# A differential-attention and SSM block on one core: TensorE turns the identity before x is ready, and two groups of waits move to later matmuls

## The reference

```
h = rmsnorm(x, g_mix);  proj = h @ w_in            # 1024 -> q, k, v, u, gate_a, gate_s
attn = diff_attention(q, k, v, rel_bias, lam, subln_g)     # 8 heads, two softmaxes each
y = s5_ssm(u, ...)                                  # diagonal state space, 32 groups
z = gelu(y) @ w_glu;  ssm = z_val * sigmoid(z_gate)
x = x + (sigmoid(gate_a) * attn + sigmoid(gate_s) * ssm) @ w_out
h = rmsnorm(x, g_mlp)
x = x + square(relu(h @ w1)) @ w2
return rmsnorm(x, g_final)
```

## Time and profile before

| | us |
|---|---|
| median of 3 runs | 754.74 (754.58 to 755.03) |
| profiled execution, its own time | 753.81 |
| span of the profiled execution | 752.0 |
| PE busy in the span | 739.0 |
| first PE instruction starts | 6.78 |
| first matmul of the first projection starts | 14.46 |

### The profile page before, as it was taken

The page is one execution under the profiler, slowest core; times in us unless marked ns, Lnnn a source line. Parts: engine busy times, 40 slices in busy tenths (PEclk is TensorE's granted clock), DMA queues, the critical chain, the costliest instruction groups (busy, mean ns, idle before and its releaser), DMA issues.

```text
span 752.0 us, 10173 instructions
## 1 busy us (share of the span) xinstructions
PE 739.0 (98%) x3826; PEld 618.0 (82%) x3826; DVE 506.8 (67%) x952; ACT 360.9 (48%) x630; POOL 54.1 (7%) x51
## 2 busy tenths in 40 slices
PE   6999999999999999999999999999999999999996
PEld 5878888888888888888888888888888888888885
DVE  4669998776667873546752576756676567647687
ACT  7524632256667664642332655434453345335455
POOL 2210000000000100000001000011000200010005
PEclk9999999999999999999999999999999999999999
DMA  7674339952224431326339563788277835795322
GB/s 248 196 164 121 93 112 173 173 143 72 71 71 127 155 113 45 89 91 224 107 90 254 134 145 85 188 241 193 64 158 244 209 104 112 196 260 131 84 58 112
DMA packets 99505, 106.19 MB, mean 141 GB/s; under 512 B 10540, under 2 KB 68576, under 8 KB 98432
## 3 DMA queue, kind: packets, MB, share of 16 engines
q1 hardware_dynamic: 93120, 87.05, 40.8%
q0 software_dynamic: 5504, 16.78, 12.0%
q10 hardware_dynamic: 832, 1.71, 1.1%
HBM read 89.70 MB, written 5.34 MB: 126 GB/s over the span
## 4 chain that ended last, share of the span: by engine, by line
PE 98%; DMA 0%; DVE 0%; ACT 0%; issue 0%; DVEq 0%
PE ps L1703 29%; PE ps L1704 29%; PE ps L1705 29%; PE ps L2018 3%; PE ps L1991 2%; PE ps L2008 1%; PE ps L1779 1%; PE ps L1787 1%; PE ps L1910 1%; PE ps L1894 1%; PE ps L1871 0%; PE ps L1914 0%; DMA mixA<-in_x 0%; PE ps L1786 0%; PE ps L1882 0%; PE ps L1859 0%
## 5 line engine op out<-in xcount | busy, mean ns | idle before, releaser
L1703 PE MATMUL ps<-hT_hi,w_hi 128*128 128x512 f32 x384 | 151.0, 393 | 0.3 <-DVE hT_lo L1038 0.3
L1705 PE MATMUL ps<-hT_hi,w_lo 128*128 128x512 f32 x384 | 149.7, 390 | 0.0
L1704 PE MATMUL ps<-hT_lo,w_hi 128*128 128x512 f32 x384 | 149.5, 389 | 0.0
L1703 PE MATMUL ps<-w_hi,hT_hi 128*128 128x512 f32 x288 | 113.7, 395 | 0.0
L1705 PE MATMUL ps<-w_hi,hT_lo 128*128 128x512 f32 x288 | 112.3, 390 | 0.0
L1704 PE MATMUL ps<-w_lo,hT_hi 128*128 128x512 f32 x288 | 112.1, 389 | 0.0
L1498 DVE TENSOR_TENSOR w_lo<-raw,w_hi 128x1024 fp32r<-128x1024 f32 x78 | 94.5, 1221 | 22.9 <-ACT w_hi L906 21.5
L906 ACT ACTIVATE w_hi<-raw 128x1024 fp32r<-128x1024 f32 x78 | 81.7, 1052 | 56.2 <-PE ps L1705 56.2
L664 ACT ACTIVATE w_hi<-raw 128x1024 fp32r<-128x1024 f32 x62 | 64.2, 1058 | 56.5 <-PE ps L1705 51.2
L1703 PE MATMUL ps<-w_hi,fa_hi 128*128 128x512 f32 x224 | 87.1, 389 | 0.0
L1704 PE MATMUL ps<-w_lo,fa_hi 128*128 128x512 f32 x224 | 87.1, 389 | 0.0
(11 more groups left out here) (271 smaller groups left out, 1030.9 us busy)
## 6 DMA issues: line engine op xcount, KB each, us to landing
raw<-in_w SPq DMA_DIRECT2D x64, 512.0 KB, 4.7
raw<-in_w_in SPq DMA_DIRECT2D x44, 512.0 KB, 5.0
raw<-raw POOLq DMA_DIRECT2D x8, 1024.0 KB, 7.1
raw<-in_w_glu SPq DMA_DIRECT2D x8, 512.0 KB, 3.8
raw<-in_w_out SPq DMA_DIRECT2D x8, 512.0 KB, 3.8
T_w<-in_w SPq DMA_DIRECT2D x8, 512.0 KB, 6.9
T_w<-in_w POOLq DMA_DIRECT2D x8, 512.0 KB, 7.7
raw<-in_w POOLq DMA_DIRECT2D x8, 512.0 KB, 6.8
```

The source lines that it names most:

```text
L1703: nc.tensor.matmul(dst, a_hi, b_hi, start=start, stop=False)
L1704: nc.tensor.matmul(dst, a_hi, b_lo, start=False, stop=False)
L1705: return nc.tensor.matmul(dst, a_lo, b_hi, start=False, stop=stop)
```

## The change

There are three edits, all in PE's list. First, a new helper turn_identity turns the identity onto itself, into a place of PSUM that the turning of x overwrites later: 24 times as soon as the identity is there, before the wait for the first block of x, and 8 times before the wait for the third. Second, the first projection's wait for the whole w_lo of unit 0 stands no longer before channel block 0 but before channel block 1; for units 1 to 3 it stands where it stood. Third, in up(0, 0) the blocks k = 4 to 7 wait for hT_hi only, do the two matmuls that read hT_hi, and then wait for hT_lo before the third. The sums are the same; of two of the three matmuls of these blocks the order is exchanged.

```
+        def turn_identity(t, n):
+            for _ in range(n):
+                nc.tensor.transpose(ps[:, turn_bank(0, 0), P * t:P * t + P], ident[:, :], ident[:, :])
+
         pe.wait_ge(ident_set, 2)
+        turn_identity(0, 24)
         for t in range(TOK):
+            if t == 2:
+                turn_identity(t, 8)
             pe.wait_ge(x_scaled, t + 1)
...
         for u in range(U_SSM, U_V):
-            pe.wait_ge(w_lo_done, u + 1)
             for t in range(TOK):
...
                     if t == 0:
+                        if u or k:
+                            pe.wait_ge(w_lo_done, u + 1)
                         pe.wait_ge(hT_lo_done, k + 1)
...
             for k in range(KT):
+                w = slice(P * k, P * k + P)
+                if c == 0 and n == 0 and k >= 4:
                     if k == 4:
                         turn(2, range(4, 8), x2, nat_added, 4 * TOK)
+                    pe.wait_ge(hT_hi_done, 2 * KT + k + 1)
+                    nc.tensor.matmul(ps[:, bank, :], w_hi[:, u % RING, w], hT_hi[:, k, :], start=False, stop=False)
+                    nc.tensor.matmul(ps[:, bank, :], w_lo[:, u % RING, w], hT_hi[:, k, :], start=False, stop=False)
                     pe.wait_ge(hT_lo_done, 2 * KT + k + 1)
+                    mm = nc.tensor.matmul(ps[:, bank, :], w_hi[:, u % RING, w], hT_lo[:, k, :], start=False,
+                                          stop=(k == KT - 1))
+                    continue
```

More of the change, by code:

```diff
@@ L2108, in up @@
             for k in range(KT):
-                if c == 0 and n == 0:
+                w = slice(P * k, P * k + P)
+                if c == 0 and n == 0 and k >= 4:
                     if k == 4:
                         turn(2, range(4, 8), x2, nat_added, 4 * TOK)
+                    pe.wait_ge(hT_hi_done, 2 * KT + k + 1)
+                    nc.tensor.matmul(ps[:, bank, :], w_hi[:, u % RING, w], hT_hi[:, k, :], start=False, stop=False)
+                    nc.tensor.matmul(ps[:, bank, :], w_lo[:, u % RING, w], hT_hi[:, k, :], start=False, stop=False)
                     pe.wait_ge(hT_lo_done, 2 * KT + k + 1)
-                w = slice(P * k, P * k + P)
+                    mm = nc.tensor.matmul(ps[:, bank, :], w_hi[:, u % RING, w], hT_lo[:, k, :], start=False,
+                                          stop=(k == KT - 1))
+                    continue
+                if c == 0 and n == 0:
+                    pe.wait_ge(hT_lo_done, 2 * KT + k + 1)
                 mm = mm3(ps[:, bank, :], w_hi[:, u % RING, w], w_lo[:, u % RING, w], hT_hi[:, k, :], hT_lo[:, k, :],
```

## The result

The changed kernel takes 762.11 us in the median of 22 runs (753.64 to 763.72); the kernel before takes 754.74 us in 22 runs beside them. The ratio is 1.0056, with a 95% interval of 1.0033 to 1.0079: slower, where 752.9 was forecast. (The quotient of the two medians is 1.0098; the ratio is nearer to 1 because the changed kernel's runs fall into two groups.) The median alone hides what the runs look like: 8 of the 22 lie between 753.64 and 755.16 (median 754.03, 0.7 us under the short runs of the kernel before), and 14 between 760.43 and 763.72. The kernel before has such long runs too, 3 of 22. The profiled execution of the changed kernel is a long one: 763.63 us, span 761.8.

What follows compares the result with a forecast made beforehand. PE, busy 739.0 of 752.0 us, was taken to bound the kernel, slow-clocked at the start. Terms 1.0 + 0.42 = 1.42, plus 0.46 for the clock's rise, off 754.74 gave 752.86, say 752.9; range 752.1 to 755.9.

Steps and rivals of the forecast that it cites:

- Edit 1: At the start: turnings raise PE's clock early, so the first projection starts at 13.45 instead of 14.46; 1.0 us.
- Edit 2: First projection: without the wait for POOL's w_lo of unit 0 it isn't held until 13.61; 0.16 us, inside the 1.0.
- Edit 3: First MLP unit: the matmul behind the sixteen turnings starts at 420.70 instead of 421.12; 0.42 us.
- Does it reach the end?: Behind the start and the MLP: PE has no other idle entry, DVE moves ahead with it, nothing takes either term back.
- a new wait later on takes it back: Sign of a wrong prediction: the first projection comes early, but a later wait, place not given, removes the gain.
- The half microsecond for the moment of the rise: Half of the 0.93 us between median and profiled time, 0.46 us, taken off for a later clock rise in timed runs.
- Rival (a): Start: turnings don't raise the clock, so the eight delay the third block 1.5 us; +1.1 us net, 755.8; chance 0.27.
- (b): Start: clock rises early but the ACT and DVE chain doesn't move; only edit 3 counts, 754.3; chance 0.04.
- (c): Start: clock rises only between 10.3 and 13.06, cost and gain offset; 754.3 within 0.7; chance 0.07.

Runs made afterwards that it cites:

- e23_act: Edits 2 and 3 without edit 1, copy of u_pairs on ScalarE, against the kernel before: 754.52 us, ratio 1.0001, 11 runs, none long.
- e23_only: Edits 2 and 3 without edit 1, copy of u_pairs on POOL, against the kernel before: 754.15 us, ratio 0.9993, 11 runs, none long.
- e1_only: Edit 1 alone, copy of u_pairs on POOL, against the kernel before: 755.27 us, ratio 1.0042, 5 of 12 runs long.
- e1_act: Edit 1 alone, copy of u_pairs on ScalarE, against the kernel before: 753.91 us, ratio 0.9990, 11 runs, none long.
- poollate_gap: before_poollate with DVE's split of w_lo moved behind the BL subtraction, so DVE waits for itself earlier: 754.78 us, ratio 0.9999 to the kernel before.
- after_act2: The changed kernel with the copy of u_pairs moved from POOL to ScalarE: 753.75 us, ratio 0.9990 to the kernel before, 1 of 11 runs long.
- after_frow: The changed kernel with ACT's store of frow issued behind its copy of C: 752.61 us, ratio 1.0000 to the kernel before, 1 of 11 long.
- after_act_frow: The changed kernel with frow's store moved behind ACT's copy of C and the u_pairs copy on ScalarE: 752.66 us, ratio 0.9985 to the kernel before.
- before_poollate: The kernel before with POOL's copy of u_pairs held until DVE is about to begin the BL block: 763.67 us, ratio 1.0124, all 4 runs long.
- after_gap: The changed kernel with DVE's split of w_lo moved behind the BL subtraction: 754.37 us, ratio 0.9998 to the kernel before, 2 of 12 long.
- after: The changed kernel, all three edits, copy of u_pairs on POOL: 762.11 us, ratio 1.0056 to the kernel before, 14 of 22 runs long.
- after_again: The changed kernel word for word, run again on another chip: 754.34 us, ratio 1.0013 to the kernel before, 2 of 12 runs long.
- after_dvewait: The changed kernel with DVE held before the BL block until the copy of u_pairs is done: 753.95 us, ratio 1.0002 to the kernel before.
- poollate_fill: before_poollate with 60 turnings of the identity on PE before its wait for u_pairs: 761.79 us, ratio 1.0094 to the kernel before.
- before_act: The kernel before with the copy of u_pairs moved from POOL to ScalarE: 754.96 us, ratio 1.0003, 11 runs.

## Why the prediction was wrong

- **Edit 1, the 32 turnings.** The mechanism was right at every step: turnings raise the clock, the first block comes at high speed, x_diag's first pass at 11.35 (forecast 11.3), hT_hi at 11.94 (11.85), hT_lo at 12.74 (12.65), the projection at 13.64 (13.45). Of the 0.2 us that are missing, 0.1 comes from x: DVE scaled the third block from 9.64, where it was 9.54. The other 0.09 is the last step: PE follows 0.90 us after hT_lo's start, in every trace with edit 2, where 0.81 was taken from the MLP. The size, 1.0 us, was read from one execution, and in others the clock rises before it matters (e23_act, e23_only). Over all profiled executions the projection starts at 13.58 in the mean of 11 with edit 1 (12.62 to 14.37, x comes at different times) and at 14.44 in the mean of 7 without (13.52 to 15.40): 0.86 us.
- **Edit 2.** 0.16 us was forecast, inside the 1.0. In e1_only and e1_act, which lack the edit, the projection starts 1.01 us after hT_lo and not 0.90, so it is worth 0.11. The reason given, that POOL's w_lo isn't done, is not shown: poollate_gap has the same 1.01, and there POOL was done 0.7 us earlier. The wait at its new place holds nothing, as forecast.
- **Edit 3.** 0.42 forecast, 0.44 in the trace. It stays to the last matmul: from turn 2 to the scale matmuls 10.48 became 10.04, and the stretch behind is 316.20 in both.
- **"Does it reach the end?" is the step that failed.** "I find nothing that takes either term back" came from the list of PE's waits and from DVE's idle time in front of its SSM work. It asked whether DVE moves with PE. DVE does; the load of u does not: the load was issued at 41.74, against 41.52 before, though its store went out 0.8 us earlier. What was never looked at is POOL's copy between them. In the kernel before, u lands at about 42.2 + 6.7 = 48.9, and DVE's last short operations end at 52.55, or at 50.85 without the 1.7 us that the copy itself held them: a margin of 1.95 us. After, they end at 50.09, 0.76 earlier, and u landed at 51.71, 2.8 later; 1.95 - 0.76 - 2.8 = -1.6 us. The copy then lasted until DVE's next gap. The gain itself took only 0.76 us of the margin; 2.8 us are the late landing, which comes with edit 1 in some executions and whose cause is open (e23_only started as early and kept the margin). An engine that doesn't wait then closed the door in front of one whose data comes by transfer. That cost 6.9 us of standing still and 2.9 us behind it at the low clock, against a gain of 1.26. The prediction named this outcome ("a new wait later on takes it back") and gave it neither a place nor a chance; it lay in the 0.15 left above the range.
- **The half microsecond for the moment of the rise.** The 0.93 us between the median and the profiled execution of the kernel before was put down to the clock or the way of measuring. It is most likely the end of the program: that profiled execution is one of two among 18 whose span ends some 6.4 us after the start of the last matmul, all others end about 7.5 after it. By its own terms the forecast would then have been 754.74 - 1.42 = 753.3.
- **Rival (a)** fell with the first row of the trace. That turnings don't raise the clock was the reading that the trace of before allowed. The Trainium skill ("TensorE: Matmul & The Clock Gate", Part 4: PE-mode transpose) says that the high clock doesn't engage for them; by that rule the eight turnings would have taken 1.7 us. They took 1.04, so here the measurement decides against it, and so does the fast third block of e23_only. (b) didn't come: the chain of ACT and DVE moved. (c) is shown by no trace with edit 1.

Where no copy was long, the change brought 0.7 us (8 of the 22 runs), 1.0 (after_act2) and 1.3 (after_frow, after_act_frow; with the store moved, and part of it perhaps the short end) in the medians, less than the forecast 1.42 in all. So even without the long copy the size was forecast too large.

## What to carry to other kernels

An edit that makes one chain earlier moves everything timed by it, but not what comes by transfer: before counting a gain, list the operations of GpSimd and ask beside which stretch of VectorE each falls, how much margin it has, and who waits for it. Where GpSimd's work must stand beside a row of two-input operations of VectorE, put a wait of VectorE for its own result early in that row, or give the work to ScalarE. The early wait made the difference between 763.67 (before_poollate) and 754.78 (poollate_gap), but it is no guarantee: after_gap still had 2 long runs of 12. And take the size of a term at the start from several executions.

## What the runs showed of the hardware

- **A copy of 128 x 2048 float32 on POOL takes 1.89 us where it gets in at once and up to 15.29 beside DVE**, not by getting slower, as it seems, but by not getting in: it ends 1.7 us after DVE starts again behind its first wait for its own result, in after, e1_only, before_poollate and poollate_gap alike. An operation of DVE behind such a wait is held 1.6 us (3.86 and 3.88 against 2.28). The Trainium skill ("SBUF — State Buffer", SBUF: two separate sides) says that GpSimd and a two-input operation of VectorE exclude each other for a whole instruction. The traces agree (1.88 instead of about 0.2 for L1184), and add what the page doesn't tell: of VectorE's operations that stood ready one behind the other, five (e1_only) to seven (after) went ahead of the waiting copy. In after_gap, after_again, after_dvewait and after_frow it got in without such a wait, within one or two operations.
- **The same meeting makes two ends of the program.** In the last 20 us POOL and DVE both add to x. In the kernel before and after_frow, two operations of DVE at L1599 took 1.30 us and two splits 2.36; in the changed kernel, as in all 15 others, one of each was held, and the end came 1.1 us later, whatever the change. That the one makes the other is read from the traces and tested by no run. Of DVE, the kernel before and the changed one:

```profile
733.66 1.30 DVE L1599 TENSOR_TENSOR x<-x,whole 128x512 f32<-128x512 f32 x2
...
736.06 2.36 DVE L1498 TENSOR_TENSOR w_lo<-raw,w_hi 128x1024 fp32r<-128x1024 f32 x2
```
```profile
742.39 2.38 DVE L1599 TENSOR_TENSOR x<-x,whole 128x512 f32<-128x512 f32 x2
...
745.90 3.44 DVE L1498 TENSOR_TENSOR w_lo<-raw,w_hi 128x1024 fp32r<-128x1024 f32 x2
```

- **The first rise of the clock without turnings of the identity** came by 10.5 in e23_only, before 11.34 in e23_act, by 11.9 in poollate_fill, at about 12.4 in poollate_gap, 13.06 in the kernel before, 14.2 in before_act and 14.8 in before_poollate; in front of each of them PE had begun the same turnings between 6.6 and 6.9 us. With the 24 turnings it was high when x came, but for after_gap, where it rose during the first block (the 24 turnings took 5.38 us, all of them slow).
- **The same load of 512 KB** (the second half of u_nat) took from 6.5 to 13.2 us to land.
